# Twelve of the fourteen projections of x become fp32r products of high and low parts, with the splitting of the weights on ACT and POOL

## The reference, cut to what matters

```python
h = rms_norm(x, norm_mix_g)
proj = h @ w_in                       # 1024 -> 2304 columns
q_sb, k_sb, v_sb, x_rg, gate_rg, q_ca = jnp.split(proj, IN_SPLITS, axis=-1)
o_sb = stick_breaking_attention(q_sb, k_sb, v_sb)      # 8 heads of 64
o_rg = gelu(gate_rg) * rg_lru(causal_depthwise_conv(x_rg))
o_ca = memory_cross_attention(q_ca, mem, ...)          # 4 heads, k and v from mem
x = x + concat(norm(o_sb), norm(o_rg), norm(o_ca)) @ w_out
x = x + moe_ffn(rms_norm(x))          # top 8 of 64 experts, and a shared one
```

## Time and profile before

| what | value |
|---|---|
| median of 3 runs | 619.62 us (619.4 to 621.31) |
| the profiled execution | 622.31 us, of which the span of its instructions 620.5 us |
| granted clock of TensorE, mean | 0.972 |
| busy: PE, PEld | 568.3 us (92%), 368.6 us (59%) |
| busy: DVE, ACT, POOL | 202.0, 139.7, 20.3 us |
| moved by DMA | 228.13 MB, mean 368 GB/s |

### The profile page before, as it was taken

How to read it: one execution, slowest core, us unless ns; L and a number is a source line. 1 busy time by engine, 2 the same in 40 slices (tenths; PEclk the granted TensorE clock), 3 DMA queues, 4 the chain that set the end, 5 groups by cost and what they waited for, 6 DMA issues and landing times.

```text
span 620.5 us, 9982 instructions
## 1 busy us (share of the span) xinstructions
PE 568.3 (92%) x4044; PEld 368.6 (59%) x4045; DVE 202.0 (33%) x516; ACT 139.7 (23%) x263; POOL 20.3 (3%) x78
## 2 busy tenths in 40 slices
PE   7999998999999998995999999899988999599775
PEld 5888774457566556662676565656655665356351
DVE  2247686777225222221222212112222122022102
ACT  4454246343111111110111101111111111011101
POOL 1003131000000000000000000000000000000000
PEclk8999999999999999997899999999999999899987
DMA  8995359633899999999999999999999999999992
GB/s 341 424 393 205 136 222 360 285 120 145 345 397 388 383 423 421 420 421 422 421 421 419 420 421 417 421 423 420 421 420 421 420 421 421 421 420 419 421 372 94
DMA packets 34143, 228.13 MB, mean 368 GB/s; under 512 B 3888, under 2 KB 4016, under 8 KB 8624
## 3 DMA queue, kind: packets, MB, share of 16 engines
q1 hardware_dynamic: 33952, 227.46, 89.5%
q10 hardware_dynamic: 144, 0.02, 0.0%
HBM read 226.42 MB, written 1.05 MB: 367 GB/s over the span
## 4 chain that ended last, share of the span: by engine, by line
PE 57%; DMA 24%; SPq 12%; ACT 2%; DVE 2%; issue 2%; ACTq 0%
DMA cell_gu<-in_w_up_e 16%; PE ps L1584 16%; SPq L355 9%; PE ps L1606 9%; PE ps L1336 7%; PE ps L1558 5%; DMA cell_gu<-in_w_gate_e 5%; PE ps L1614 5%; PE ps L1458 4%; PE ps L1353 4%; DMA cell_d<-in_w_down_e 2%; PE ps L1505 2%; PE ps L1343 1%; SPq L452 1%; DMA wA<-in_w_qk 1%
## 5 line engine op out<-in xcount | busy, mean ns | idle before, releaser
L1584 PE MATMUL ps<-cell_gu,xg 128*64 128x256 f32 (+2 forms) x2048 | 196.6, 404 | 30.2 <-DMA cell_gu<-in_w_up_e 20.0
L1584 PEld LDWEIGHTS ps<-cell_gu,xg 128*64 128x64 f32 (+2 forms) x2048 | 127.5, 133 | 106.0 <-issue 59.0
L1606 PE MATMUL ps<-cell_d,e_hT 128*64 128x512 f32 (+2 forms) x512 | 96.6, 611 | 5.0 <-issue 3.6
L1221 DVE TENSOR_TENSOR e_h<-e_sg,ps 128x256 f32<-128x256 f32 x26 | 16.1, 619 | 197.2 <-ACT e_sg L754 197.2
L1282 DVE SCALAR_TENSOR_TENSOR ylo<-ps,gslot,yhi 128x512 fp32r<-128x512 f32 x52 | 39.0, 751 | 121.7 <-ACT yhi L768 121.7
L1606 PEld LDWEIGHTS ps<-cell_d,e_hT 128*64 128x64 f32 (+2 forms) x512 | 28.2, 127 | 59.1 <-issue 56.4
L768 ACT ACTIVATE yhi<-ps,gslot 128x512 fp32r<-128x512 f32 x52 | 35.7, 687 | 121.8 <-PE ps L1606 121.8
L754 ACT ACTIVATE e_sg<-ps 128x256 f32<-128x256 f32 x26 | 10.0, 384 | 219.8 <-PE ps L1584 219.8
L1558 PE MATMUL ps<-pick,xhi 128*128 128x256 f32 x208 | 45.3, 299 | 1.1 <-DVE pick L1139 1.1
L1614 PE MATMUL ps<-yhi,S 128*128 128x512 f32 x104 | 43.3, 417 | 0.6 <-DVE ylo L1282 0.6
L1558 PE MATMUL ps<-pick,xlo 128*128 128x256 f32 x208 | 41.9, 283 | 0.0
(11 more groups left out here) (315 smaller groups left out, 496.6 us busy)
## 6 DMA issues: line engine op xcount, KB each, us to landing
cell_gu<-in_w_gate_e SPq DMA_DIRECT2D x64, 1024.0 KB, 26.2
cell_gu<-in_w_up_e SPq DMA_DIRECT2D x64, 1024.0 KB, 26.6
cell_d<-in_w_down_e SPq DMA_DIRECT2D x60, 1024.0 KB, 27.2
wA<-in_w_qk SPq DMA_DIRECT2D x8, 512.0 KB, 10.6
wo<-in_w_out SPq DMA_DIRECT2D x1, 4096.0 KB, 13.3
cell_d<-in_w_down_e SPq DMA_DIRECT2D x8, 512.0 KB, 17.3
wR<-in_w_rest SPq DMA_DIRECT2D x3, 1024.0 KB, 28.0
wV<-in_w_v SPq DMA_DIRECT2D x1, 2048.0 KB, 17.6
```

The lines of the kernel that those rows point to most:

```text
L1221: nc.vector.tensor_tensor(dst[:].rearrange("q k p -> q p k"), e_sg[:].rearrange("q (p k) -> q p k", k=KH), ps[:, U, DE:2 * DE].rearrange(" ...
L1584: last = mm(ps[side * w:(side + 1) * w, U, cols], rows(k, slice(side * w, (side + 1) * w)), cell_gu[i][:, k, :], start=k == 0, stop=k == K ...
L1606: last = mm(ps[side * w:(side + 1) * w, Y[half], :], e_hT[:, kk, side * w:(side + 1) * w], cell_d[n][:, kk, half * 512:(half + 1) * 512], ...
```

## The change

Of the projections of x that were plain fp32, units 0 and 1 stay so, and ten units (2 to 7, 10, 11, 14 to 17) become fp32r products of parts; with the two units of v (8, 9), which were so before, that makes twelve. For each chunk, one matmul of 512 columns multiplies the high part of the weights by both parts of x, which now lie side by side (`h_both`), into the two halves of the bank, and one of 256 columns adds the low part of the weights by the high part of x to the first half. (In units 10 and 11 x is the stationary operand, and the parts of the weights lie side by side.) So:

- ACT casts the high parts of each weight block (`split_q` of 128x1024 for units 2 to 7, `split_r` of 128x2048 for `wR[2]`, `wR[0]`, `wR[1]`), and POOL subtracts for the low parts, as one instruction of 128x1024 for each `split_q` and two for each `split_r`. They stand in the walk; POOL's share of a split comes between its masks.
- DVE adds the two halves of a bank with a `reduce_sum` over 512 PSUM elements before its multiply, which now reads SBUF. Unit 10's evacuation moves from ACT to DVE.
- The high parts of the weights lie in the place of cells 16 and 17, low parts overwrite the weights. The first loads of the cells are reordered around this: gate and up of expert 1 go to cells 6 and 7 and wait for units 0, 1 and the split of x; gate and up of 4 follow `wo`; those of 3 and down of 1 and 2 wait for unit 17.
- Some semaphores are merged. POOL's first writes of `rest` come later, before its masks of head 0.

```diff
-        walk = [("unit", 0), ("unit", 1), ("row", 0), ("unit", 2), ("unit", 3), ("unit", 4), ("split_w", 0), ("unit", 5),
-                ("split_w", 1), ("unit", 6), ("mem_norm", 0), ("unit", 7), ("split_a", 1)]
+        walk = [("unit", 0), ("unit", 1), ("split_q", 2), ("row", 0), ("split_q", 3), ("unit", 2), ("split_q", 4), ("unit", 3),
+                ("split_q", 5), ("split_q", 6), ("unit", 4), ("split_w", 0), ("split_q", 7), ("unit", 5), ("split_w", 1), ("unit", 6),
+                ("mem_norm", 0), ("unit", 7), ("split_r", 2), ("split_a", 1)]
...
-            walk += {2: [("split_w", 2)], 3: [("split_w", 3)], 5: [("log1p", 0)], 7: [("ca_square", 0)], 8: [("ca_norm", 0)], 9: [("conv", 0)],
+            walk += {2: [("split_w", 2)], 3: [("split_w", 3)], 5: [("split_r", 0), ("log1p", 0)], 6: [("split_r", 1)], 7: [("ca_square", 0)], 8: [("ca_norm", 0)], 9: [("conv", 0)],
...
+            sp.wait_ge(unit_ps, 2)
+            sp.wait_ge(alo_dve, 1)
             load_fixed("gate", 1)
+            sp.wait_ge(ssq_act, 2)
             load_fixed("up", 1)
...
             sp.wait_ge(unit_ps, 10)
-            load_fixed("down", 1)
             load_fixed("gate", 2)
             load_fixed("up", 2)
...
             sp.dma_start(wo[:], w_out).then_inc(wo_loaded, 16)
+            load_fixed("gate", 4)
+            load_fixed("up", 4)
...
+            sp.wait_ge(unit_ps, 18)
+            load_fixed("down", 1)
+            load_fixed("down", 2)
+            load_fixed("gate", 3)
+            load_fixed("up", 3)
...
+            def split_q(n):
+                pool.wait_ge(win_hi_act, n - 1)
+                pool.tensor_tensor(wA_lo[n][:], wA[n][:], wA_hi[n % 4][:].bitcast(F32), ALU.subtract).then_inc(win_lo_pool, 1)
+
+            def split_r(g):
+                pool.wait_ge(win_hi_act, (8, 9, 7)[g])
+                for c in (slice(0, 4), slice(4, 8)):
+                    hi, lo = (w2_both[:, 0, c, :], w2_both[:, 1, c, :]) if g == 2 else (wR_hi[g][:, c, :], wR_lo[g][:, c, :])
+                    pool.tensor_tensor(lo, wR[g][:, c, :], hi.bitcast(F32), ALU.subtract).then_inc(win_lo_pool, 1)
...
+            def split_q(n):
+
+                act.wait_ge(wA_loaded[n], 16)
+                if n >= 6:
+                    act.wait_ge(unit_ps, n - 3)
+                nc.scalar.copy(wA_hi[n % 4][:], wA[n][:]).then_inc(win_hi_act, 1)
+
+            def split_r(g):
+
+                act.wait_ge(wR_loaded[g], 16)
+                act.wait_ge(unit_ps, 8 if g == 2 else 12)
+                nc.scalar.copy(w2_both[:, 0] if g == 2 else wR_hi[g][:], wR[g][:]).then_inc(win_hi_act, 1)
...
+                    src = b[:, 0:SEQ]
+                    if n in IN_PARTS:
+                        src = dst
+                        link(nc.vector.reduce_sum(src, b.rearrange("p (i s) -> p s i", i=2), AX.X))
+                    nc.vector.tensor_tensor(dst, src, rstd_row[:], ALU.mult).then_inc(unit_dve, 1)
...
+                        pe.wait_ge(win_lo_pool, 10 + 2 * g)
+                        hi, lo = wR_hi[g], wR_lo[g]
+                    for k in range(KD):
+                        mm(b, hi[:, k, c:c + P], h_both[:, :, k, :], start=k == 0, stop=k == KD - 1, skip_group_check=True)
+                        last = mm(b[:, 0:SEQ], lo[:, k, c:c + P], hT_hi[:, k, :], start=False, stop=k == KD - 1,
+                                  skip_group_check=True)
```

More of the change, by code:

```diff
@@ L132, in hybrid_decoder_layer @@
     wA = [at(f"wA{n}", o_A + 4 * KB * n, [P, KD, P]) for n in range(8)]
+    wA_lo = [at(f"wA_lo{n}", o_A + 4 * KB * n, [P, KD, P], F32R) for n in range(8)]
+    wA_hi = [at(f"wA_hi{b}", o_more + 4 * KB * b, [P, KD, P], F32R) for b in range(4)]
+    w2_both = at("w2_both", o_more, [P, 2, KD, CA], F32R)
     wo = at("wo", o_A, [P, KD, D])
@@ L138, in hybrid_decoder_layer @@
     wR = [at(f"wR{g}", o_R + 8 * KB * g, [P, KD, 256]) for g in range(3)]
+    wR_lo = [at(f"wR_lo{g}", o_R + 8 * KB * g, [P, KD, 256], F32R) for g in range(2)]
+    wR_hi = [at(f"wR_hi{g}", o_more + 8 * KB * g, [P, KD, 256], F32R) for g in range(2)]
     r = Space(o_R)
@@ L418, in _ @@
             load_shared("up")
-            load_fixed("down", 2)
             sp.wait_ge(unit_ps, 20)
-            for e in (3, 4):
-                for part in ("gate", "up", "down"):
-                    load_fixed(part, e)
+            load_fixed("down", 3)
+            load_fixed("down", 4)
             sp.wait_ge(unit_ps, 26)
@@ L507, in _, with edges @@
             pool.memset(grp[:], HUGE).then_inc(consts, 1)
[L509 to L516, removed]
+            def edges():
+                pool.wait_ge(xT_act, KD // 2)
+                pool.wait_ge(xT_dve, KD // 2)
+                pool.wait_ge(alo_dve, 1 + KD)
+                for b in range(2):
+                    link(pool.memset(rest[b][:, P:P + 1], 1.0))
+                    last = pool.memset(rest[b][:, NZ + 1:NZ + 2], 1.0)
+                    link(last)
+                pool.memset(stat[:, 15:16], 0.0).then_inc(zeroed, 1)
+            def split_q(n):
[6 more added lines that the diff above has]
+                    pool.tensor_tensor(lo, wR[g][:, c, :], hi.bitcast(F32), ALU.subtract).then_inc(win_lo_pool, 1)
             for kind, h in walk:
+                if kind == "split_q":
+                    split_q(h)
+                elif kind == "split_r":
+                    split_r(h)
                 if kind != "z":
                     continue
+                if h == 0:
+                    edges()
                 pool.wait_ge(bc_act, 2 * h + 2)
@@ L630, in split_a @@
                     act.wait_ge(xT_dve, KD // 2)
-                    nc.scalar.copy(hT_hi[:], hT[:]).then_inc(ahi_act, 1)
+                    nc.scalar.copy(hT_hi, hT[:]).then_inc(ahi_act, 1)
             def split_w(i):
@@ L655, in _ @@
                     split_w(n)
+                elif kind == "split_q":
+                    split_q(n)
+                elif kind == "split_r":
+                    split_r(n)
                 elif kind == "mem_norm":
@@ L861, in evac @@
                 elif n < 12:
-                    dst, src, rms = ca_raw[:, 0, n - 10, :], b[:, 0:CA], stat[:, n - 8:n - 7]
+                    dst, src, rms = ca_raw[:, 0, n - 10, :], ca_raw[:, 0, n - 10, :], stat[:, n - 8:n - 7]
+                    link(nc.vector.reduce_sum(src, b.rearrange("p (i s) -> p s i", i=2), AX.X))
                 elif n < 14:
```

58 lines of the change are left out of this document (31 added, 27 removed).

## The result

| | median | range | runs |
|---|---|---|---|
| kernel before, same chip | 620.45 us | 619.4 to 621.31 | 4 |
| changed kernel | 638.14 us | 637.16 to 640.92 | 4 |

The ratio is 1.0292 (1.0259 to 1.0325): the change makes the kernel 2.9% slower, 17.7 us, where 7.4 were forecast and 633.0 was the top of the range. The profiled execution took 640.92 us, with a span of 639.2.

The account below looks back on a forecast made before the run. The mixer's end, fixed by two equal chains (PE's; masks of head 6 plus DVE), sets when the weight-bound experts start. Masks +5.95 and two sums +1.44 gave +7.4 on 619.6: 627.0 us, range 620.5 to 633.0.

Parts of the forecast that it names:

- The frame: Whole kernel: experts run at their weights' pace, so if the mixer ends X later, the kernel ends X later.
- PE's gain is lost: At unit 20, which reads `xc` behind DVE's `conv`: a gain on PE alone, 0.68 us a unit, is lost.
- The terms of the new work: New units: PE saves 0.68 us each, 6.8 for ten; POOL's 128x1024 subtraction costs 2.36 us, DVE's sum 0.72 with its link.
- Does POOL wait for DVE?: POOL and DVE sharing SBUF: POOL stops while DVE reads two SBUF inputs, and DVE is not delayed.
- rival (a): DVE waits for POOL, first come; masks of head 6 +9.8, in all +11.9, 631.5 us; chance 0.26.
- Unit 6 waits 4.7 us for POOL.: Units 2 to 7: POOL's part of 6 is done at 33.7, and unit 7 ends at 39.3, 1.8 us later.
- Head 0's scores +2.5.: Behind unit 7: the parts of `mem` end at 45.4, so head 0's scores start 2.5 us later than 42.97.
- Unit 14 waits 2.7.: Units 14 and 16: POOL's low part of `wR[0]` is done at 76.0, so unit 14 waits 2.7 us.
- Masks of head 6 at +5.95, for which DVE waits.: Before `conv`: masks queue behind POOL's split of `wR[1]`, end at 84.25 against 78.3; DVE's scan waits for them.
- Two sums, 1.44.: DVE's stretch without idle time before `conv`: two `reduce_sum`, of units 15 and 16, add 1.44 us.
- The clock: Left out of the sum: unit 6's wait of 4.7 us may bring the lower clock again, +1.7 us.
- every rival: Four alternatives: DVE waits for POOL, 0.26; no mutual delay, 0.13; faster POOL, 0.06; partial delay, 0.09.

Follow-up runs that it names:

- run 7: Changed kernel with only units 2 to 7 in parts, low parts subtracted by DVE instead of POOL, `log1p` moved early: 619.15 us, ratio 0.9981.
- run 9: Changed kernel with only units 2 to 7 in parts, their low parts still on POOL and `log1p` in its place: 620.26 us, ratio 1.0014.
- run 10: Changed kernel with each POOL subtraction cut into two of 128x512: 638.33 us, ratio 1.0296.
- run 12: Kernel before with two unused 128x1024 POOL subtractions ahead of the masks of head 5 and two ahead of head 6's, each pair waiting for DVE: 625.22 us.
- run 5: Changed kernel without the sums of bank halves on DVE; each multiply reads the first half from PSUM: 631.85 us, ratio 1.0191.
- Run 6: Changed kernel with the split of `wR[2]` moved behind the parts of `mem`, on ACT and POOL: 632.98 us, ratio 1.0203.
- run 2: Changed kernel with the `log1p` chain moved from step 5 to before unit 8's evacuation: 633.29 us, ratio 1.0215.
- run 1: Changed kernel with each POOL subtraction replaced by two memsets that write the same low part and read nothing: 624.72 us, ratio 1.0073.
- run 8: Changed kernel, all twelve in parts, with low parts on DVE, the split of `wR[2]` behind the parts of `mem`, then `log1p`: 624.34 us, ratio 1.0072.

## Why the prediction was wrong

**The frame held.** "If the mixer ends X later, the kernel ends X later" is the table above. That PE's gain is lost was right in the main: runs 7 and 9 keep six of the cheaper units, 6 x 0.63 = 3.8 us of PE, and end within 0.3% of the kernel before. In run 7's trace `conv` does end 2.8 us earlier, but its median is only 1.0 us lower. The windows of the long stretch of experts show the same clock (0.97) and the same DMA (418 and 419 GB/s) as before.

**The terms of the new work held, one count did not.** Sixteen units project x (0 to 11 and 14 to 17), and fourteen of them were plain before; it is of these fourteen that twelve (2 to 7, 10, 11, 14 to 17) go into parts, without v's. The section on the change and the prediction count them as ten, so by the prediction's own price PE saves 12 x 0.68 = 8.2 us on paper, not 6.8. The sum doesn't use that total, since it lays the units out one by one; it has no effect on the 7.4. Starts of one chunk and the next are 0.353 us apart in the new units (0.3465 forecast), POOL's 128x1024 takes 2.35 to 2.60, in the mean 2.47 (2.36), the sum 0.69 and its multiply starts 0.70 to 0.73 behind it (0.72).

**The step that failed** is the one under "Does POOL wait for DVE?": "POOL stops while DVE reads two SBUF inputs, and DVE is not delayed." The second half is wrong. It rested on a row in which DVE had been first and on selects that last 0.27 us each. That DVE's scans "went on as usual" beside those selects is not quite what the kernel before shows. Its last product beside the selects, and that of the next head, where POOL is idle:

```profile
48.45 0.51 DVE L948 TENSOR_TENSOR beta<-beta,rest 128x256 f32<-128x256 f32 x1
...
51.44 0.42 DVE L948 TENSOR_TENSOR beta<-beta,rest 128x256 f32<-128x256 f32 x1
```

The product took 0.51 us instead of the 0.42 that it takes for every other head: a trace of a hold, too short to price. The change itself, run 10 and run 12 show that DVE waits for the running POOL subtraction, for up to 2.3, 1.2 and 1.75 us as that one is long. The first half of the sentence held: in run 5 a POOL subtraction that came second took 4.48 us. The sentence of the Trainium skill (SBUF — State Buffer, "Who interferes with whom") that issue order decides and the other side blocks for the whole instruction agrees with these rows; the measured +17.7 stands nearer to the +11.9 of rival (a), which was that rule, than to the forecast.

What followed from it, in the prediction's order:

- *Unit 6 waits 4.7 us for POOL.* It didn't: POOL came first and wasn't slowed, its last subtraction for these units ended at 30.9, and unit 7 ended at 35.2 instead of 39.3. DVE paid instead, 2.2 us in `wV_lo` and 3.0 in three multiplies by `rstd_row` that now read two SBUF operands.
- *Head 0's scores +2.5.* Measured +5.8 (rival (a) had +6.8): `memT_lo` stretched by 3.9. Run 6 takes this wait away, moving ACT's cast and POOL's subtractions of `wR[2]` alone, and ends 4.9 us better.
- *Unit 14 waits 2.7.* 2.6: right, but no longer the path.
- *Masks of head 6 at +5.95, for which DVE waits.* The masks came at 88.3, but DVE wasn't idle for them; it was behind with its own work. Run 12 shows such a wait: its second pair of subtractions meets an idle DVE, and the scans of head 6 wait for POOL 4.8 us, in part by the wait that was added there.
- *Two sums, 1.44.* Mis-sized: as DVE didn't wait for the masks of head 6, the sum of unit 14 counts as well, and between 28.5 and 37.3 us DVE has no idle time either, so that the sums there delay `memT_lo`. Run 5 puts the sums at 6.0 us, together with the waits that the multiply has because it now reads SBUF.
- *The clock*, +1.7 left out of the sum. The lower level came after PE's waits at head 0 (0.61 from 44 to 51 us) and at the recurrence's gates (3.67 us instead of 1.94).

**What was overlooked in every rival.** `log1p` was no term of any sum, as it is 25 instructions of 0.16 to 0.22 us on two columns. With POOL's subtractions beside it it takes 6.4 us more, and moving it away gains 3.9 (run 2). Rival (a) had the right mechanism and +11.9. It puts the end of the masks of head 6 9.8 us late, at 88.1, and they ended at 88.3; but DVE came to them only at 93.76. What kept it is this chain (6.4) and the product of head 4 ahead of it (2.2), which rival (a) lacked.

**How the 17.7 us divide.** By run 1, 12.5 of them go away when POOL writes without reading. Of the other 5.2, its trace shows 1.3 at the end of `conv` and 1.7 at the gates, which run at the lower level of the clock. By run 8, with no POOL subtraction and in another order, 13.5 go away. The 4.2 that stay are what nine more blocks to cast on ACT and to subtract on DVE, and twelve sums, cost beyond PE's gain; its rows show 3.0 at the end of `conv` and 1.5 at the gates (3.45 us instead of 1.94), and a wait for `w_kv_lo` with the clock behind it of 3.6 in all, of which it was not tested how much reaches the end. The single savings of runs 2, 5 and 6 (3.9, 6.0, 4.9) overlap with each other and with run 1's and must not be added to it. What the clock at head 0 costs by itself was not separated, nor was POOL's length in run 1 (1.9 instead of 2.4 us a block). Not tried: the chain on `lam` kept in PSUM.

## What to carry to other kernels

Work moved to an idle POOL isn't free: while it subtracts in SBUF, a DVE instruction between SBUF operands can take as long as a whole POOL instruction (2.3 us here), however small it is. So count the DVE instructions that fall beside it, not their microseconds; a chain of tiny ones is the worst neighbour, and cutting POOL's work into halves didn't help (run 10). A row in which the other engine came first, or in which the holder is short, says little of who waits for whom. And before a busy engine's unit is made cheaper, walk every other engine's list to the end of the stage: here PE saved 12 x 0.63 = 7.6 us and DVE, the second equal chain, got the bill.

## What the runs showed that was not expected

- The hold has two kinds. POOL's subtraction, which reads and writes SBUF, held DVE's TENSOR_TENSOR, scan and TENSOR_SCALAR (rows of 1.98 to 2.61 us) and SCALAR_TENSOR_TENSOR (7.14 for eight). POOL's memset, which only writes, held TENSOR_SCALAR (0.85) and let TENSOR_TENSOR (0.16) and SCALAR_TENSOR_TENSOR (3.29 for eight) pass. The same section of the Trainium skill parts the two cases so: a DVE instruction with two SBUF inputs contends with a GpSimd one that reads SBUF and not with one that only writes it; one in a two-port mode, which it says `tensor_scalar` can enter, contends with GpSimd without that limit. These rows agree, down to instructions of two elements a partition, though no view shows the mode that an instruction ran in.
- The copy of `yT` from PSUM (78.51, 0.41 us) and `reduce_sum` from PSUM (0.68 to 0.69 us throughout) ran beside POOL's subtractions unharmed, and so did the multiply with its source in PSUM (0.42 in run 5, 2.12 from SBUF). RECIPROCAL on 128x2 kept its 0.17 us beside POOL's subtractions in runs 10 and 12 and inside a memset in run 1.
- POOL's subtraction took 2.4 us with two different operands and 1.93 with both operands the same block (run 12); the output's type differed too, so which of the two makes the difference is open.
